# Two-layer decoder trunk: layer 0's first weight tiles on two queues, its keys gathered earlier, its gathered rows stored by GpSimd

## The chip, the cores and the metric

The kernel runs on one core of one Trainium2 chip. The metric is the device time of one execution in microseconds (us). A core has these engines: PE (TensorE, matmuls; PEld is its weight load), DVE (VectorE), ACT (ScalarE), POOL (GpSimd) and SP (SyncE). All data between DRAM and the on-chip memory, and from DRAM to DRAM, is moved by the core's 16 DMA engines. Three engines issue such transfers here, each into a queue of its own: SP (q1 in the profile), ACT (q10) and POOL (q0). Each queue is served in the order in which it was filled.

## What is computed

Two layers over 256 prompt positions and 8 sample rows which share the weights. Cut to what matters here (the function and variable names are the reference's):

```python
h = rms_norm(x, norm_g)
proj = jnp.einsum('btd,de->bte', h, w_in)            # 1024 -> 3200 columns
...                                                  # conv group, pooling group
kk = jnp.concatenate([k_buf, k], axis=1)             # cache of 2048 keys + the new one
vv = jnp.concatenate([v_buf, v], axis=1)
o = dilated_attention(q, kk, vv, k_buf.shape[1])     # dilations (1, 4, 16), 128 keys each
new_k = kk[:, -n_keep:]                              # the whole cache, shifted by one row
new_v = vv[:, -n_keep:]
y = jnp.einsum('bte,ed->btd', jnp.concatenate([ya, yb, yc], axis=-1), w_out)
```

The sample group's outputs `new_k` and `new_v` are the caches of both layers moved by one row: 8 samples, 2 layers, keys and values, 2048 rows of 1536 bytes each. That shifted copy is most of what the kernel moves.

## The kernel before, in words

**Weights.** There are 66 weight tiles of 128 rows of 4096 bytes (512 KB), 33 a layer: 25 projections (`PROJ`, in the order a_val and a_glu alternating, a_gate, q, k, v, c_gate, b_val, b_gate) and 8 output tiles. They go through a ring of `WRING = 14` buffers `wt`. SP issues tiles 0 to 13 at the start (L435), with most of the constants (`cst`, L437) behind the sixth; ACT issues tile n + 14 after it has drained projection n (`next_tile`, L786). PE multiplies tile by tile (L596 projections, L739 outputs) into three PSUM banks `pj`.

**Gathered rows.** Each layer's attention of the samples needs 20 slots of rows in `kg` (keys) and 20 in `vg` (values). `gather` issues 24 DMAs for each: 8 for the nearest rows (16 partitions x 4 slots, two rows of 1536 bytes in one piece of 3072: 64 pieces) and 16 for dilations 4 and 16 (16 x 6 slots of 1536 bytes: 96 pieces). DVE multiplies `kg` with the query `qb` (L1098, step `sscore`); in its order stands the rotary part of the next k tile (L1028 and after) behind the first of these products, and PE waits for that. PE reads `vg` in L668.

**The shifted copy.** POOL issues 96 copies from DRAM to DRAM (L511; three a sample: 256, 240 and 96 pieces of 4608 bytes; layer 1's first, then layer 0's) and 4 remainders (L515). They leave out the near rows and every fourth row of the part behind them; those come from `kg` and `vg`, by `put_back` (16 DMAs each: 8 with 64 pieces, 8 with 96), which SP issues (L406).

**SP's order, one instruction after the other.** x and constants, tiles, keys of layer 0, then in each layer: pool weights `pw`, `gather("v", l)` (its buffer `vg` holds x at the start; in layer 1 it waits until layer 0's values are stored), the states, `put_back` of the keys, parameters and states of the next layer, `gather("k", 1)` once layer 0's keys are used and stored, `put_back` of the values. At the end SP stores y and waits for all that is outstanding.

Of the kernel before, what the change touches and what calls it, by code (L numbers as in the profile page):

```python
# [37 lines left out]
PER_S = P // NS  # L38
# [7 lines left out]
GATHER = []  # L46
# [4 lines left out]
    _hi = _lo  # L51
SLOTS = sum(g[2] for g in GATHER)
NEW = SLOTS
SCORE_CUTS = [(a, a + 4) for a in range(0, SLOTS, 4)]


# [38 lines left out]
assert NRING % RING == 0  # L95

WRING = 14


CONV_TAPS = CONV_W * CT  # L100
# [79 lines left out]
          for a, b in ((0, 768), (768, EVEN_ROWS), (FAR_LO, GATHER[0][0]))]  # L180
NEAR_BYTES = 2 * C_ATT * 4
IN_FLIGHT = 16
assert DEPTH * len(COPIES) % IN_FLIGHT == 0
XROUNDS = 5

# [60 lines left out]
def trunk_program(nc, ins, const, const_at, outs):  # L246
    (y_prompt, y_sample, o_conv_p, o_pool_p, o_k_p, o_v_p, o_conv_s, o_pool_s, o_k_s, o_v_s) = outs
    with ExitStack() as ctx:
# [92 lines left out]
        for name, n in dict(  # L341

                par_in=10 * 16, st_in=2 * 16, pw_in=4 * 16, k_in=3 * NS * 16, v_in=3 * NS * 16,

                k_near_out=NS * 16, k_far_out=NS * 16, v_near_out=NS * 16, v_far_out=NS * 16, v_out=16, k_out=16, new_out=4 * 16, tail_out=4 * 16, state_out=2 * 16,

                pj_full=NRING, pj_free0=NRING // RING, pj_free1=NRING // RING, pj_free2=NRING // RING,
                tr_full=NTR, tr_free=NTR, st_full=NST, st_free=NST, rt_full=NRT, rt_free=NRT,
                sc_full=NH + 1, sc_free=NH + 1, o_full=NH, o_free=AT,

                xsq=KD, r_h_ok=1, h_ok=KD, qk_raw=2 * AT, qk_r=2 * AT, qk_ok=2 * AT,
                v_raw=AT, rep_ok=3, sig_ok=NGATES, u_ok=CT, sig_c_ok=AT, sig_a_ok=CT, sig_b_ok=PT_,
                nmax_ok=NH, p_raw=NH, p_ok=NH, kprod_ok=len(SCORE_CUTS), ks_used=len(SCORE_CUTS), ssub=1, sexp=1, spm_ok=1, so_ok=1,
                conv_ok=CONV_TAPS, yc_ok=1,
                ysq=1, rstd_ok=1, z_ok=1, ztanh=1, b_val_ok=PT_, pd_ok=1,
                mix_a=1, mix_b=PT_, mix_c=AT, mix_s=1, xT_ok=KD).items():
            S[name] = sem(name)
            per[name] = n
# [20 lines left out]
        def tile_of(g):  # L379

            return wt[:, g % WRING, :, :].rearrange("p k c -> p (k c)"), ins["w_tiles"][g // NRING, g % NRING], w_in[g % WRING]

        @block.sync
        def _(sp):
            def one(name, l):
                return ins[name][bass.ds(l, 1)]

            def gather(kind, l, to, name):

                at = 0  # L390
                for lo, d, n in GATHER:
                    for s in SAMPLE_ORDER:
                        rows = one(f"cache_{kind}_win", l)[:, s, lo:lo + d * n * PER_S]
                        rows = rows.rearrange("o (a b e) h d -> (o a) b e (h d)", a=PER_S, e=d)[:, :, 0, :]
                        sp.dma_start(to[sample_rows(s), at:at + n, :], rows, max_dma_last_dim=NEAR_BYTES).then_inc(S[name], 16)  # L395
                    at += n

            def put_back(l, to, frm, names):

                out = to[bass.ds(l, 1)]  # L400
                at = 0
                for (lo, d, n), name in zip(GATHER, names):
                    for s in SAMPLE_ORDER:
                        rows = out[:, s, lo - 1:lo - 1 + d * n * PER_S]
                        rows = rows.rearrange("o (a b e) h d -> (o a) b e (h d)", a=PER_S, e=d)[:, :, 0, :]
                        sp.dma_start(rows, frm[sample_rows(s), at:at + n, :], max_dma_last_dim=NEAR_BYTES).then_inc(S[name], 16)  # L406
                    at += n

            def params(l):
                sp.wait_ge(S["tr_full"], nth(l - 1, "tr_full", TR["par"] + 1))  # L410
# [19 lines left out]
            sp.dma_start(x_tok[0:NS, 2 * D_MODEL:3 * D_MODEL],  # L430
                         ins["x_sample"].rearrange("s t d -> (s t) d")).then_inc(x_in, 16)
            sp.dma_start(cst[:, 0:early], const[:, 0:early]).then_inc(early_in, 16)
            for g in range(WRING):
                buf, src, landed = tile_of(g)
                sp.dma_start(buf, src).then_inc(landed, 16)  # L435
                if g == 5:
                    sp.dma_start(cst[:, early:], const[:, early:]).then_inc(const_in, 16)  # L437

            for l in range(DEPTH):

                if l == 0:
                    gather("k", l, kg, "k_in")
                sp.wait_ge(zeroed, 1)
                if l > 0:
                    sp.wait_ge(S["rt_full"], nth(l, "rt_full", 0))
                for g in range(len(POOL_WINDOWS)):
                    r = 64 * (g % 2)
                    sp.dma_start(pw[r:r + 64, g // 2, r:r + 64], one("pool_w", l)[:, g].rearrange("o c d -> (o c) d"))\
                        .then_inc(S["pw_in"], 16)

                if l == 0:
                    sp.wait_ge(x_copied, XROUNDS)
                    sp.wait_ge(squared, 1)
                else:
                    sp.wait_ge(S["sc_full"], nth(l - 1, "sc_full", NH + 1))
                    for name in ("v_near_out", "v_far_out"):
                        sp.wait_ge(S[name], nth(l - 1, name, per[name]))
                sp.wait_ge(S["pj_full"], nth(l, "pj_full", PIDX[("a_gate", 0)]))
                gather("v", l, vg, "v_in")
                for name, out, keep in (("state_conv", o_conv_s, TAIL - 1), ("state_pool", o_pool_s, POOL_BUF - 1)):  # L460
                    sp.dma_start(out[bass.ds(l, 1), :, 0:keep].rearrange("o s w c -> (o s) (w c)").rearrange("s (e x) -> e s x", e=16),
                                 one(name, l)[:, :, 1:keep + 1].rearrange("o s w c -> (o s) (w c)").rearrange("s (e x) -> e s x", e=16))\
                        .then_inc(S["state_out"], 16)

                sp.wait_ge(S["k_in"], nth(l, "k_in", per["k_in"]))
                sp.wait_ge(S["pj_full"], nth(l, "pj_full", PIDX[("v", 0)]))
                put_back(l, o_k_s, kg, ("k_near_out", "k_far_out"))
                if l < DEPTH - 1:
                    params(l + 1)
                    states(l + 1)  # L470
                    sp.wait_ge(S["ks_used"], nth(l, "ks_used", len(SCORE_CUTS)))
                    for name in ("k_near_out", "k_far_out"):
                        sp.wait_ge(S[name], nth(l, name, per[name]))
                    gather("k", l + 1, kg, "k_in")
                sp.wait_ge(S["v_in"], nth(l, "v_in", per["v_in"]))
                put_back(l, o_v_s, vg, ("v_near_out", "v_far_out"))
            y_rows = y_prompt.rearrange("b (r p) d -> r p (b d)", p=P)
            sp.wait_ge(y_copied, 1)
            sp.dma_start(y_rows[0][:, 0:512], y_tok[:, 0:512]).then_inc(y_out, 16)
# [8 lines left out]
            sp.wait_ge(bulk_out, 16 * 4)  # L488
            for i in range(IN_FLIGHT):
                sp.wait_ge(copy_out[i], 16 * DEPTH * len(COPIES) // IN_FLIGHT)  # L490
            for name in ("k_near_out", "k_far_out", "v_near_out", "v_far_out", "v_out", "k_out", "new_out", "tail_out", "state_out"):
                sp.wait_ge(S[name], DEPTH * per[name])
            sp.wait_ge(y_out, 80)

# [1 line left out]
        def _(pool):  # L496
# [4 lines left out]
            for l in reversed(range(DEPTH)):  # L501
                for i, (kind, s, a, b) in enumerate(COPIES):
                    n = (DEPTH - 1 - l) * len(COPIES) + i
                    cache, out = (ins["cache_k_win"], o_k_s) if kind == "k" else (ins["cache_v_win"], o_v_s)
                    if a < FAR_LO:
                        dst = out[l, s, a:b].rearrange("(c e r) h d -> c e (r h d)", c=16, r=PIECE_ROWS)
# [251 lines left out]
        def _(act):  # L758
# [9 lines left out]
            for r0, name in ((ROW_QN, "q_norm_g"), (ROW_KN, "k_norm_g")):  # L768
                for h in range(2):
                    act.dma_start(prow[r0:r0 + 1, h * HD:(h + 1) * HD], ins[name][bass.ds(0, 1)]).then_inc(S["par_in"], 16)  # L770

            act.wait_ge(x_in, 32)
            act.wait_ge(early_in, 16)
            unused = hT[:, :, :].rearrange("p k c -> p (k c)")
# [3 lines left out]
            A(mix[0:NS, :, :].rearrange("p k c -> p (k c)")[:, 0:D_MODEL], x_tok[0:NS, 2 * D_MODEL:3 * D_MODEL], ACT.Square,  # L778
              accum_out=x_sum[0:NS, 2:3]).then_inc(squared, 1)
            act.wait_ge(squared, 1)  # L780

            def next_tile(g):

                if g < DEPTH * NRING:
                    buf, src, landed = tile_of(g)
                    act.dma_start(buf, src).then_inc(landed, 16)  # L786

            act.dma_start(st_conv[:, :, :], ins["state_conv"][bass.ds(0, 1)].rearrange("o (r s) w c -> (o s w) r c", r=2)
                          ).then_inc(S["st_in"], 16)
            act.dma_start(st_pool[:, :], ins["state_pool"][bass.ds(0, 1)].rearrange("o s w c -> (o s w) c")).then_inc(S["st_in"], 16)  # L790
            for l in range(DEPTH):
                def rsqrt_of(dst, src, scale, free_n, ok_sem, n):

# [5 lines left out]
                for step in ACT_SCHEDULE:  # L799
# [17 lines left out]
                    elif kind == "proj":  # L817
# [30 lines left out]
                        elif group == "b_val":  # L848
                            nc.scalar.copy(p_ext[:, t, POOL_BUF:], src[:, 0:SEQ])
                            nc.scalar.copy(p_smp[:, t, :, POOL_BUF], src[:, SEQ:T]).then_inc(S["b_val_ok"], 1)  # L850
                            act.wait_ge(S["b_val_ok"], nth(l, "b_val_ok", t + 1))
                            act.sem_inc(free, 1)
                        next_tile(l * NRING + n + WRING)
                    elif kind == "norm":
                        i = step[1]
# [409 lines left out]
```

## Time and profile before

| what | us |
|---|---|
| median of three runs | 409.22 (408.93 to 413.0) |
| the profiled execution, device time | 406.74 |
| its span, first to last instruction | 404.9 |
| PE busy | 336.8 |
| DVE busy | 232.5 |
| ACT busy | 99.3 |
| POOL busy | 54.2 |

All times in the rows are us from the start of the span. The profiled execution lies 2.5 us below the median of the three runs, and 1.8 us lie around its span. The page gives the busy time of each engine, the span in 40 slices with the share in which the 16 DMA engines were busy and the rate in GB/s, the DMA queues, and the chain of work that ended last. A DMA queue's "packets" are the pieces that it moved, with the small ones that report a transfer's end. SPq, ACTq and POOL's DMA rows are the times in which those engines issue transfers.

### The profile page before, as it was taken

How to read it: one execution, taken by the hardware profiler on the slowest of the kernel's cores; microseconds unless marked ns; L12 is line 12 of the kernel's file. 1: busy time of each engine (PE TensorE's matmuls, PEld its weight loads, DVE VectorE, ACT ScalarE, POOL GpSimd, SP SyncE). 2: the span in 40 equal slices, each digit the busy share in tenths (PEclk: the TensorE clock that was granted, in tenths of full speed). 3: DMA queues.
4: the chain of work that ended last, by engine and by line, in shares of the span. 5: the costliest groups of instructions: out<-in, count | busy, mean ns of one | idle time of the engine just before them, and what ended most of it. 6: DMA issues, size and time to landing. Idle time of an engine off the chain costs nothing.

```text
span 404.9 us, 4681 instructions
## 1 busy us (share of the span) xinstructions
PE 336.8 (83%) x1546; PEld 267.5 (66%) x1546; DVE 232.5 (57%) x524; ACT 99.3 (25%) x234; POOL 54.2 (13%) x104
## 2 busy tenths in 40 slices
PE   1799999920557897898997999999778996989991
PEld 1588888810435675667886888888556765758881
DVE  1625798401998578753103358988988587662101
ACT  2300215410023333251102001353214332340011
POOL 2710101111111111111011110111111011200000
PEclk9999999975595999999999999999867999999997
DMA  7999999999999999999999999999999999999995
GB/s 289 417 419 419 419 418 416 416 415 379 363 396 394 395 404 414 411 367 393 415 418 417 412 417 418 415 414 386 416 416 383 387 375 399 359 399 359 345 330 196
DMA packets 51269, 158.10 MB, mean 390 GB/s; under 512 B 6356, under 2 KB 18078, under 8 KB 51246
## 3 DMA queue, kind: packets, MB, share of 16 engines
q0 software_dynamic: 21056, 89.61, 56.7%
q1 hardware_dynamic: 20804, 38.60, 25.8%
q10 hardware_dynamic: 9386, 29.60, 18.3%
q8 instruction: 12, 0.20, 0.2%
q14 instruction: 11, 0.09, 0.1%
HBM read 143.91 MB, written 104.42 MB: 613 GB/s over the span
## 4 chain that ended last, share of the span: by engine, by line
PE 49%; DVE 19%; SPq 18%; DMA 6%; ACT 3%; issue 3%; ACTq 0%; DVEq 0%
PE pj L596 21%; PE pj L739 14%; SPq L395 14%; DMA kg<-in_cache_k_win 6%; DVE yc L1157 4%; SPq L435 4%; PE psc L668 4%; DVE tok L1098 3%; DVE ssc L1101 3%; PE ptr L521 3%; DVE spsum_pad L1127 1%; PE ps L716 1%; PE ps L555 1%; ACT sc L903 1%; DVE sc L1065 1%
## 5 line engine op out<-in xcount | busy, mean ns | idle before, releaser
L596 PE MATMUL pj<-hT,wt 128*128 128x264 f32 x800 | 194.1, 401 | 3.0 <-DVE hT L1017 3.0
L596 PEld LDWEIGHTS pj<-hT,wt 128*128 128x128 f32 x800 | 156.6, 199 | 34.7 <-issue 7.3
L1157 DVE SCALAR_TENSOR_TENSOR yc<-u_ext,par,yc 128x256 f32<-128x256 f32 x180 | 76.2, 480 | 2.8 <-DVE u_smp L1045 0.6
L739 PE MATMUL pj<-mix,wt 128*128 128x264 f32 x256 | 59.4, 387 | 0.0
L739 PEld LDWEIGHTS pj<-mix,wt 128*128 128x128 f32 x256 | 48.0, 190 | 7.9
L511 POOL DMA_DIRECT2D out<-in_cache_v_win x48 | 25.8, 544 | 166.0 <-issue 166.0
L511 POOL DMA_DIRECT2D out<-in_cache_k_win x48 | 26.0, 549 | 119.4 <-issue 111.8
L1227 DVE TENSOR_TENSOR xT<-xT,pj 128x264 f32<-128x264 f32 x16 | 6.9, 430 | 53.5 <-PE pj L739 53.5
L1098 DVE TENSOR_TENSOR tok<-kg,qb 128x1536 f32<-128x1536 f32 x10 | 17.6, 1758 | 23.4 <-DMA kg<-in_cache_k_win 22.9
L608 PE MATMUL prt<-sqg,cst 128*128 128x264 f32 x24 | 7.9, 415 | 22.2 <-DVE scr L1028 22.2
L844 ACT ACTIVATE ex<-pj 128x264 f32<-128x264 f32 x22 | 8.6, 391 | 69.6 <-PE pj L596 56.0
L608 PEld LDWEIGHTS prt<-sqg,cst 128*128 128x128 f32 x24 | 4.7, 200 | 23.3 <-DVE scr L1028 22.6
L1101 DVE TENSOR_REDUCE ssc<-tok 128x24 f32<-128x1536 f32 x10 | 17.5, 1753 | 0.3
L521 PE MATMUL ptr<-cst,sc 128*128 128x128 f32 x36 | 7.0, 310 | 12.3 <-DVE sc L1076 12.3
L802 ACT ACT_TABLE_LOAD x12 | 15.4, 1283 | 1.6 <-ACT sqg L831 0.9
L1043 DVE SCALAR_TENSOR_TENSOR u_ext<-ex,pj 128x256 f32<-128x256 f32 x6 | 2.5, 422 | 22.2 <-ACT ex L844 22.2
L668 PE MATMUL psc<-vg,spm_pad 128*64 128x384 f32 x80 | 15.2, 502 | 0.0
L521 PEld LDWEIGHTS ptr<-cst,sc 128*128 128x128 f32 x36 | 4.4, 153 | 16.0 <-DVE sc L1076 15.6
L1052 DVE SCALAR_TENSOR_TENSOR mix<-ex,pj 128x264 f32<-128x264 f32 x16 | 6.9, 428 | 9.5 <-ACT ex L844 9.3
L951 ACT ACTIVATE hT<-xT 128x264 f32<-128x264 f32 x8 | 3.4, 422 | 31.7 <-DVE xT L1227 31.7
L901 ACT ACTIVATE sc<-sc,nmax 128x128 f32<-128x128 f32 x12 | 4.8, 401 | 25.2 <-DVE nmax L1069 19.3
L835 ACT COPY vT<-pj 128x264 f32<-128x264 f32 x6 | 2.3, 379 | 35.4 <-PE pj L596 35.3
(175 smaller groups left out, 329.3 us busy)
## 6 DMA issues: line engine op xcount, KB each, us to landing
wt<-in_w_tiles ACTq DMA_DIRECT2D x52, 512.0 KB, 8.1
out<-in_cache_k_win POOLq DMA_DIRECT2D x16, 1152.0 KB, 66.2
out<-in_cache_v_win POOLq DMA_DIRECT2D x16, 1152.0 KB, 61.4
out<-in_cache_k_win POOLq DMA_DIRECT2D x17, 1080.0 KB, 70.7
out<-in_cache_v_win POOLq DMA_DIRECT2D x17, 1080.0 KB, 64.7
wt<-in_w_tiles SPq DMA_DIRECT2D x14, 512.0 KB, 21.6
out<-in_cache_k_win POOLq DMA_DIRECT2D x16, 432.0 KB, 72.5
out<-in_cache_v_win POOLq DMA_DIRECT2D x16, 432.0 KB, 66.7
```

Of the source, the lines that this page charges most:

```text
L395: sp.dma_start(to[sample_rows(s), at:at + n, :], rows, max_dma_last_dim=NEAR_BYTES).then_inc(S[name], 16)
L435: sp.dma_start(buf, src).then_inc(landed, 16)
L511: pool.dma_start(dst, src, max_dma_last_dim=PIECE_ROWS * C_ATT * 4).then_inc(copy_out[n % IN_FLIGHT], 16)
L521: return nc.tensor.transpose(out, in_, C["ident"][0:rows, 0:rows])
L596: last = nc.tensor.matmul(pj[n % RING][:, 0:T], wt[:, g % WRING, k, :], hT[:, k, :], start=(k == 0), stop=(k == KD - 1))
L608: nc.tensor.matmul(prt[:, 0:T], C["rot"], qg[:, i % 2, :], start=True, stop=True).then_inc(S["rt_full"], 1)
L668: nc.tensor.matmul(psc[o:o + SV_HALF, 0:C_ATT], spm_pad[:, j * NH * NS:j * NH * NS + SV_HALF], v, start=(j < 2), stop=(j >= SLOTS - 1))
L739: last = nc.tensor.matmul(pj[n % RING][:, 0:T], wt[:, g % WRING, k, :], mix[:, k, :], start=(k == 0), stop=(k == KD - 1))
L802: nc.scalar.preload_act_table_set(TABLE_BEFORE[step])
L1098: V.tensor_tensor(tok[:, :, :], kg[:, a:b, :], qb[:, None, :].to_broadcast([P, b - a, C_ATT]), ALU.mult).then_inc(S["kprod_ok"], 1)
L1101: last = V.tensor_reduce(ssc[:, a:b, :], tok[:, :, :].rearrange("p j (h d) -> p j h d", h=NH), AX.X, ALU.add)
L1157: last = V.scalar_tensor_tensor(out=yc[:, t, 0:SEQ], in0=x_w, scalar=par[:, ROW_CW + w * CT + t:ROW_CW + w * CT + t + 1], in1=yc[:, t, 0:S ...
```

## The change

Four edits. SP issues only tiles 0 to 3, then the 8 near gathers of layer 0's keys, then the constants, then the 16 others. ACT issues tiles 4 and 5 before it waits for x, tiles 6 to 9 behind the first states, and 10 to 13 after it has drained projection 0. `put_back` takes the engine that issues it; for layer 0 that is POOL, which stores the keys ahead of its 25th copy and the values ahead of its 49th, each behind a wait for the gather (`k_in`, `v_in`). Layer 1's rows are stored by SP as before, on semaphores of their own.

```diff
+SP_TILES, ACT_TILES = 4, (6, 10)
+STORED = {"k": 3 * NS, "v": 6 * NS}
...
-            for g in range(WRING):
+            for g in range(SP_TILES):
                 buf, src, landed = tile_of(g)
                 sp.dma_start(buf, src).then_inc(landed, 16)
-                if g == 5:
-                    sp.dma_start(cst[:, early:], const[:, early:]).then_inc(const_in, 16)
+            gather("k", 0, kg, "k_in", GATHER[:1])
+            sp.dma_start(cst[:, early:], const[:, early:]).then_inc(const_in, 16)
+            gather("k", 0, kg, "k_in", GATHER[1:])
...
-                if l == 0:
-                    gather("k", l, kg, "k_in")
...
-                sp.wait_ge(S["k_in"], nth(l, "k_in", per["k_in"]))
-                sp.wait_ge(S["pj_full"], nth(l, "pj_full", PIDX[("v", 0)]))
-                put_back(l, o_k_s, kg, ("k_near_out", "k_far_out"))
+                if l > 0:
+                    sp.wait_ge(S["k_in"], nth(l, "k_in", per["k_in"]))
+                    put_back(sp, l, o_k_s, kg, ("k_near_last", "k_far_last"))
...
-                sp.wait_ge(S["v_in"], nth(l, "v_in", per["v_in"]))
-                put_back(l, o_v_s, vg, ("v_near_out", "v_far_out"))
+                if l > 0:
+                    sp.wait_ge(S["v_in"], nth(l, "v_in", per["v_in"]))
+                    put_back(sp, l, o_v_s, vg, ("v_near_last", "v_far_last"))
...
+                    if n == STORED["k"]:
+                        pool.wait_ge(S["k_in"], nth(0, "k_in", per["k_in"]))
+                        put_back(pool, 0, o_k_s, kg, ("k_near_out", "k_far_out"))
+                    elif n == STORED["v"]:
+                        pool.wait_ge(S["v_in"], nth(0, "v_in", per["v_in"]))
+                        put_back(pool, 0, o_v_s, vg, ("v_near_out", "v_far_out"))
...
+            for g in range(SP_TILES, ACT_TILES[0]):
+                next_tile(g)
             act.wait_ge(x_in, 32)
...
+            for g in range(*ACT_TILES):
+                next_tile(g)
...
+                        if l == 0 and n == 0:
+                            for g in range(ACT_TILES[1], WRING):
+                                next_tile(g)
                         next_tile(l * NRING + n + WRING)
```

SP's first instructions before (`vg` holds x at the start, `kg` the gathered keys, `wt` the weight tiles; the numbers behind are partitions, slots and elements):

```order
L428 DMA vg<-in_x_prompt 128x2x1024
L430 DMA vg<-in_x_sample 8x1024
L432 DMA cst<-in_const 128x129
L435 DMA wt<-in_w_tiles 128x1024 x6
L437 DMA cst<-in_const 128x1279
L435 DMA wt<-in_w_tiles 128x1024 x8
L395 DMA kg<-in_cache_k_win 16x4x768 x8
L395 DMA kg<-in_cache_k_win 16x6x384 x16
```

And SP's first instructions of the change:

```order
L431 DMA vg<-in_x_prompt 128x2x1024
L433 DMA vg<-in_x_sample 8x1024
L435 DMA cst<-in_const 128x129
L438 DMA wt<-in_w_tiles 128x1024 x4
L410 DMA kg<-in_cache_k_win 16x4x768 x8
L440 DMA cst<-in_const 128x1279
L410 DMA kg<-in_cache_k_win 16x6x384 x16
```

Ten tiles have gone from SP's queue, and the near keys stand ahead of the constants. ACT's part of the change, from its first tile on (`prow` and `st_*` are parameters and states, `ex` the gate of projection 1):

```order
L780 DMA prow<-in_k_norm_g 1x64 x2
L786 DMA wt<-in_w_tiles 128x1024 x2
L794 ACTIVATE hT,x_sum<-vg 128x1024 x2
L796 ACTIVATE mix,x_sum<-vg 8x1024
L799 DMA st_conv<-in_state_conv 120x2x384
L801 DMA st_pool<-in_state_pool 120x256
L786 DMA wt<-in_w_tiles 128x1024 x4
L807 ACTIVATE r_h<-ps,cst 128x264
L809 ACTIVATE r_h<-r_h 128x264
L815 ACT_TABLE_LOAD
L786 DMA wt<-in_w_tiles 128x1024 x5
L857 ACTIVATE ex<-pj1 128x264
```

The ten tiles stand in three places, the last four with tile 14 in one run of five ahead of `ex`. POOL's row in the change where its copies of layer 1's keys end and those of the values begin:

```order
L521 DMA out<-in_cache_k_win 96x1152
L395 DMA out<-kg 16x4x768 x8
L395 DMA out<-kg 96x1x384 x8
L521 DMA out<-in_cache_v_win 256x1152
```

The 16 stores of the keys have moved from SP to here; the 16 of the values stand in the same way ahead of the copies of layer 0.

## Rows read from the trace of the kernel before

**Rows 1.** The page's DMA and PE lines over the span's 40 slices.
```profile
PE   1799999920557897898997999999778996989991
...
DMA  7999999999999999999999999999999999999995
GB/s 289 417 419 419 419 418 416 416 415 379 363 396 394 395 404 414 411 367 393 415 418 417 412 417 418 415 414 386 416 416 383 387 375 399 359 399 359 345 330 196
DMA packets 51269, 158.10 MB, mean 390 GB/s; under 512 B 6356, under 2 KB 18078, under 8 KB 51246
```
**Rows 2.** The page's DMA queues over the span: POOL's q0, SP's q1, ACT's q10.
```profile
q0 software_dynamic: 21056, 89.61, 56.7%
q1 hardware_dynamic: 20804, 38.60, 25.8%
q10 hardware_dynamic: 9386, 29.60, 18.3%
...
HBM read 143.91 MB, written 104.42 MB: 613 GB/s over the span
```
**Rows 3.** Timeline of POOL's issues: start, length, line, transfer, idle time before.
```profile
61.20 1.61 POOL L511 DMA_DIRECT2D out<-in_cache_v_win  x3 [15.18 <-issue]
...
154.63 1.61 POOL L511 DMA_DIRECT2D out<-in_cache_k_win  x3 [11.75 <-issue]
...
348.50 1.07 POOL L515 DMA_DIRECT2D out<-in_cache_v_win  x2
```
**Rows 4.** The page's DMA issues: KB each, median us from issue to landing.
```profile
out<-in_cache_v_win POOLq DMA_DIRECT2D x16, 1152.0 KB, 61.4
...
out<-kg SPq DMA_DIRECT2D x16, 192.0 KB, 24.5
```
**Rows 5.** DMA queues in 378 to 394 us: packets, MB, share.
```profile
DMA packets 1507, 5.27 MB, mean 329 GB/s; under 512 B 134, under 2 KB 289, under 8 KB 1507
...
q0 software_dynamic: 1075, 4.57, 88.5%
q1 hardware_dynamic: 432, 0.70, 14.9%
```
**Rows 6.** Waits of SP's queue over the span: total, times, longest.
```profile
SPq L457 <- DMA out<-vg: 19.7, 1, 19.7
SPq L483 <- ACT hT L962: 11.5, 1, 11.5
SPq L473 <- DMA out<-kg: 8.3, 1, 8.3
SPq L493 <- DMA out<-qk: 4.8, 1, 4.8
```
**Rows 7.** Timeline of DVE: start, length, line, form, idle time before it.
```profile
76.66 0.56 DVE L1058 COPY qb<-ptr 128x384 f32<-128x384 f32 x1
100.11 1.76 DVE L1098 TENSOR_TENSOR tok<-kg,qb 128x1536 f32<-128x1536 f32 x1 [22.89 <-DMA kg<-in_cache_k_win]
```
**Rows 8.** Stretches: PE, PEld, DVE, ACT, POOL busy, PEclk, DMA share, GB/s.
```profile
20.00:80.00 60.00, 60.00 (x277) 50.90 (x276) 39.87 (x100) 14.72 (x36) 6.47 (x12) 1.00 1.03 418
...
100.00:112.00 12.00, 6.29 (x18) 4.87 (x18) 11.65 (x16) 0.00 (x0) 1.63 (x3) 0.58 1.01 366
112.00:180.00 68.00, 56.12 (x271) 40.93 (x271) 51.16 (x111) 23.58 (x62) 9.68 (x18) 0.92 1.03 398
180.00:280.00 100.00, 96.71 (x449) 80.68 (x448) 52.53 (x130) 21.59 (x49) 12.94 (x25) 1.00 1.03 412
280.00:380.00 100.00, 88.21 (x405) 66.28 (x404) 66.89 (x141) 28.00 (x71) 10.28 (x20) 0.91 1.03 386
...
394.00:400.00 6.00, 2.74 (x15) 1.85 (x13) 1.12 (x2) 1.05 (x2) 0.00 (x0) 1.00 0.88 329
```
**Rows 9.** DMA queues in 40 to 70 us.
```profile
q0 software_dynamic: 1221, 5.23, 42.4%
q10 hardware_dynamic: 1194, 4.23, 34.5%
q1 hardware_dynamic: 1221, 3.03, 25.4%
```
**Rows 10.** DMA queues in 0 to 10 us.
```profile
q1 hardware_dynamic: 885, 2.82, 76.7%
```
**Rows 11.** DMA queues in 10 to 40 us.
```profile
q1 hardware_dynamic: 1406, 5.24, 42.9%
q0 software_dynamic: 1174, 5.07, 41.0%
q10 hardware_dynamic: 857, 2.21, 18.5%
```
**Rows 12.** Timeline of SP's issues.
```profile
5.56 13.21 SPq L435 DMA_DIRECT2D wt<-in_w_tiles  x8
18.81 58.56 SPq L395 DMA_DIRECT2D kg<-in_cache_k_win  x24
```
**Rows 13.** Timeline of ACT around its first tile issue.
```profile
23.41 0.37 ACTq L786 DMA_DIRECT2D wt<-in_w_tiles  x1
26.97 0.39 ACT L844 ACTIVATE ex<-pj 128x264 f32<-128x264 f32 x1 [8.65 <-PE pj L596]
```
**Rows 14.** The chain that ended last: start, length, engine, line.
```profile
166.09 2.58 PE psc L668 x15
...
278.39 1.77 DVE tok L1098
...
345.34 2.82 PE psc L668 x15
...
396.98 0.59 ACT hT L962
```
**Rows 15.** DMA queues in 77 to 100 us, all together.
```profile
DMA packets 3285, 9.25 MB, mean 402 GB/s; under 512 B 585, under 2 KB 1568, under 8 KB 3285
```

More of the change, by code:

```diff
@@ L53 @@
 NEW = SLOTS
+SLOT_OF = {g[1]: sum(h[2] for h in GATHER[:i]) for i, g in enumerate(GATHER)}
 SCORE_CUTS = [(a, a + 4) for a in range(0, SLOTS, 4)]
@@ L343, in trunk_program @@
                 par_in=10 * 16, st_in=2 * 16, pw_in=4 * 16, k_in=3 * NS * 16, v_in=3 * NS * 16,
-                k_near_out=NS * 16, k_far_out=NS * 16, v_near_out=NS * 16, v_far_out=NS * 16, v_out=16, k_out=16, new_out=4 * 16, tail_out=4 * 16, state_out=2 * 16,
+                k_near_out=NS * 16, k_far_out=NS * 16, v_near_out=NS * 16, v_far_out=NS * 16,
+                k_near_last=NS * 16, k_far_last=NS * 16, v_near_last=NS * 16, v_far_last=NS * 16, v_out=16, k_out=16, new_out=4 * 16, tail_out=4 * 16, state_out=2 * 16,
                 pj_full=NRING, pj_free0=NRING // RING, pj_free1=NRING // RING, pj_free2=NRING // RING,
@@ L381, in tile_of, with put_back @@
             return wt[:, g % WRING, :, :].rearrange("p k c -> p (k c)"), ins["w_tiles"][g // NRING, g % NRING], w_in[g % WRING]
+        def put_back(eng, l, to, frm, names):
+            out = to[bass.ds(l, 1)]
+            at = 0
+            for (lo, d, n), name in zip(GATHER, names):
+                for s in SAMPLE_ORDER:
+                    rows = out[:, s, lo - 1:lo - 1 + d * n * PER_S]
+                    rows = rows.rearrange("o (a b e) h d -> (o a) b e (h d)", a=PER_S, e=d)[:, :, 0, :]
+                    eng.dma_start(rows, frm[sample_rows(s), at:at + n, :], max_dma_last_dim=NEAR_BYTES).then_inc(S[name], 16)
+                at += n
         @block.sync
@@ L386, in one, with gather @@
                 return ins[name][bass.ds(l, 1)]
-            def gather(kind, l, to, name):
-                at = 0
-                for lo, d, n in GATHER:
+            def gather(kind, l, to, name, spans=GATHER):
+                for lo, d, n in spans:
+                    at = SLOT_OF[d]
                     for s in SAMPLE_ORDER:
@@ L395, in gather @@
                         sp.dma_start(to[sample_rows(s), at:at + n, :], rows, max_dma_last_dim=NEAR_BYTES).then_inc(S[name], 16)
[L396 to L407, printed above, removed]
             def params(l):
@@ L490, in _ @@
                 sp.wait_ge(copy_out[i], 16 * DEPTH * len(COPIES) // IN_FLIGHT)
-            for name in ("k_near_out", "k_far_out", "v_near_out", "v_far_out", "v_out", "k_out", "new_out", "tail_out", "state_out"):
+            for name in ("k_near_out", "k_far_out", "v_near_out", "v_far_out", "k_near_last", "k_far_last", "v_near_last", "v_far_last"):
+                sp.wait_ge(S[name], per[name])
+            for name in ("v_out", "k_out", "new_out", "tail_out", "state_out"):
                 sp.wait_ge(S[name], DEPTH * per[name])
@@ L770, in _, with next_tile @@
                     act.dma_start(prow[r0:r0 + 1, h * HD:(h + 1) * HD], ins[name][bass.ds(0, 1)]).then_inc(S["par_in"], 16)
+            def next_tile(g):
+                if g < DEPTH * NRING:
+                    buf, src, landed = tile_of(g)
+                    act.dma_start(buf, src).then_inc(landed, 16)
+            for g in range(SP_TILES, ACT_TILES[0]):
+                next_tile(g)
             act.wait_ge(x_in, 32)
@@ L780, in _ @@
             act.wait_ge(squared, 1)
[L782 to L786, printed above, removed]
             act.dma_start(st_conv[:, :, :], ins["state_conv"][bass.ds(0, 1)].rearrange("o (r s) w c -> (o s w) r c", r=2)
```

## Prediction, made before the changed kernel ran

> **What bounds the kernel now.** The page's 40 slices come first. PE has a hole in slices 9 to 11 and again near slice 29, so PE alone isn't the bound; the DMA line stands at 9 (90% or more) from the second slice to the last but one [rows 1]. The reader is to see that the 16 DMA engines have something to do from about 10 us until 400 us, whatever the compute engines do. The queues say what: 89.61 of 158.10 MB are POOL's copies from DRAM to DRAM, each byte of which is read and written, hence 143.91 MB read and 104.42 written [rows 2]. POOL issues its last copy at about 349 us, and a copy takes some 61 us from issue to landing [rows 3, 4]: 349 + 61 = 410, so the copies run to the very end. In 378 to 394 us q0 has 88.5% of the engines' time, long after the last weight tile [rows 5]. So two things end together: the chain of compute, whose last y store SP waits for (4.8 us) [rows 6], and the copies.
>
> The waits come next. The largest on the chain of compute is DVE's for layer 0's gathered keys: the query copy at 76.66 us is done at 77.2, the product starts at 100.11, 22.89 us later [rows 7]. Everything behind it is late by that.
>
> The stretches show that the DMA engines are full at different rates: 418 GB/s in 20 to 80 us, when the tile queue is active beside the copies; 366 in 100 to 112, when all 14 buffers have filled up during DVE's wait; 412 in 180 to 280; 386 in 280 to 380; and 329 when the copies are nearly alone [rows 5, 8]. The share is about 1.0 in each, so what differs is what the pieces cost: copies want loads beside them.
>
> **Edits at the start: when do the keys land?** In 40 to 70 us all three queues have work, and their packets are 1221, 1221 and 1194 [rows 9]: the engines take a piece from each queue in turn, whatever its size. So what counts for the keys is the number of pieces ahead in SP's queue. Before: 264 for x, 256 for constants, 14 x 128 for tiles, 8 x 64 + 16 x 96 = 2048 for keys, 4360 in all, and 16 small ones for each of 42 DMAs: 5032. The change takes out ten tiles with 10 x (128 + 16) = 1440, leaving 3592. By 10 us 885 had passed [rows 10]; tiles 4 and 5 now run on ACT's queue at that time, so I take off half of their 256 pieces, leaving 757. The remaining 2835 at 1406 / 30 = 46.9 per us [rows 11] take 60 us, at 1221 / 30 = 40.7 per us [rows 9] 70 us. The keys land between 70 and 80 us; the upper end is the likelier, since ACT's queue is now full from the start, and a transfer's last engine may be some us behind the mean. They are needed at 77.2. Of the 22.9 us of wait I take 20 as gone, with 15 and 22.9 as ends.
>
> The weight tiles: ACT's queue gets its turns too. A tile is 144 packets, so 3.1 to 3.5 us at these rates; tile 6 is issued near 12 us and PE needs it some 22 us after its first. They come in time. ACT's run of five tiles at about 23.4 us can block ACT, as SP's eight tiles took 13.21 us to issue when its queue was full [rows 12]; `ex` at 26.97 stands behind them [rows 13]. By that row a blocked tile costs 13.21 / 8 = 1.65 us on average, 8 us for five, against 0.37 for one that finds room; between 0 and 8, I take 3, most of it covered by the three `pj` banks, and it is hidden anyway if the copies set the end.
>
> **POOL's stores.** POOL reaches copy 24 at 61.20 and copy 48 at 154.63 us [rows 3]. The wait for the keys holds it from 61 until 80; its queue holds 61 us of copies, so the DMA engines don't run dry: cost nothing, cover 61 against 19. Without that cover it would be the 19. The values are gathered right behind the keys (2048 + 24 x 16 pieces at 40.7 per us: 60 us, so by 140); PE reads them at 166 before, which becomes 146 [rows 14]. Each store set adds 16 x 0.54 us of issue on POOL (1.61 / 3 for one), hidden in waits of 11 to 15 us. What it moves is time of landing: instead of 24.5 us from issue a store now takes about 61 [rows 4]. Keys: issued from 80, landed by 145; layer 1's keys are needed at 278 - 20 = 258 [rows 14]. Values: issued near 165, landed by about 230; SP waited 19.7 us for this store before, until 277 [rows 6], so this comes earlier. Behind it are the values of layer 1, needed at 345 - 20 = 325 [rows 14]. No term.
>
> **The sum.** Compute ends 20 us earlier, near 377 instead of 397 [rows 14], and its y stores by 385. But the bytes are the same 158.10 MB. In those 20 us the engines moved 402 GB/s [rows 15], 8.0 MB. These have to be moved at the end instead, by copies alone: 8.0 / 0.329 [rows 5] = 24.4 us. That is +4.4 us. Against it stands the stretch of full buffers: 12 us at 366 become a stretch like 180 to 280 at 412 [rows 8], 12 x (412 - 366) / 412 = 1.3 us back. Sum +3.1 us. The other bound: the 8.0 MB spread over the late stretch at 386: 20.7 us, +0.7, less 1.3, -0.6. Between -0.6 and +3.1 I take +1.5: some of the loads and stores that now lie beside copies (SP's 25.8%) stay beside them. Span 404.9 + 1.5 = 406.4, device time 408.2 by the profiled execution. That execution is 2.5 us below the median of 409.22, so for a median: 410.7.
>
> HBM's own limit can be weighed here. In 378 to 394 us, 88% of a 329 GB/s stretch is copies, which is about 2 x 0.29 + 0.04 = 0.62 TB/s read and written [rows 5]. The Trainium skill (HBM Reference, Specifications (TRN2)) gives about 716 GB/s for the memory that two cores share. By that figure copies alone would do 358 GB/s, the 8.0 MB 22.4 us, and the sum would be +1.1 us; the trace shows less than the page's figure in that stretch, and the sum above goes by the trace.
>
> **Rivals.**
>
> 1. *The copies decide, at no price or a small one* (0.50), as above: 410.7, own range 406 to 413.
>
> 2. *Slower: the copies alone are dearer than I take.* Compute is out of the way for the full 22.9 us, 9.25 MB are moved at the end at 329 GB/s: 28.1 us, +5.2 with nothing given back: 414.4. In 394 to 400 us the DMA share already falls to 0.88 [rows 8], engines finish unevenly, and a longer stretch of copies alone may spread them further. For it: the last stretches fall from 359 to 330 GB/s [rows 1]. Against: the gather of the values beside copies without tiles ran at 366, and that goes away. It decides from +4.1 us on, that is 8.0 MB moved below 332 GB/s with nothing regained. 0.25.
>
> 3. *Faster: the mix gets better.* Stores in POOL's queue take turns in place of copies, not beside them, and tiles flow steadily. If 112 to 180 us went from 398 to 412 GB/s that is 68 x 14 / 412 = 2.3 us, and 280 to 380 from 386 to 400, 3.5 us: -5.8, 403.4. For it: every stretch with tiles shows 412 to 418. Against: layer 1's stores stay where they are, and what pauses the tiles there is DVE, not the keys. 0.20.
>
> 4. *The change doesn't bring the keys forward.* They would land near 100 and the time stays 409.2. Against: equal turns [rows 9], with 1440 packets less ahead. 0.05. The Trainium skill (DMA: Bandwidth & Descriptors, Issuing engines are not separate DMA queues) says that issuing from several engines only saves sequencer time, the transfers sharing the same 16 engines. Taken alone that gives this case; the trace's equal packet counts of three queues speak against it for one queue's landing, and for it where the sum of all bytes is meant.
>
> If DMA did not bind, the time would be 409.2 - 20 = 389; the DMA line leaves that no chance beyond what the range's low end cuts off.
>
> **How the numbers follow.** About 1% (4.1 us) is what a measurement of this kernel can tell from no change. Case 3 lies mostly on the faster side, with a little of case 1: 0.22. Case 2 mostly slower, with a little of case 1: 0.27. The rest, 0.51, is the same. The range takes in 403 (case 3) and 416 (case 2 with the spread of the runs before): 402.5 to 416.5.
>
> **What would show it.** In the profile after: DVE's wait for the keys (before its first product with `kg`) below 8 us, with keys landed by 85; PE's last matmul near 375 to 380; q0 nearly alone, at 320 to 345 GB/s, for the last 20 to 30 us rather than 15; SP's last wait for a copy, not for the y store; DMA share 9 to the last slice. Wrong if the 16 DMA engines show idle time in the middle (POOL's queue dry behind a wait), if a tile is late in 20 to 80 us, or if the copies at the end run above 360 GB/s: then the time falls below 405.

## The result, and the profile after

Over 20 runs each, the kernel before took 409.11 us (median) and the changed kernel 412.86 us. The ratio is 1.0104, with a 95% interval of 1.0084 to 1.0124: the change costs about 1%, or 4.3 us. The forecast was 410.7 us with no measurable change as the likeliest; the sign and the range (402.5 to 416.5) hold, and the time lies between the likeliest case and the slower rival. The profiled execution has a span of 411.5 us against 404.9; it lies 0.5 us above its median and the one before 2.4 us below, so the two traces show more difference than the medians.

The first look goes to the page's slices of the changed kernel (PE's busy tenths, the DMA engines' busy tenths, GB/s).

```profile
PE   2799999976999698999799999878896998994000
...
DMA  8999999999999999999999999999999999999992
GB/s 292 415 418 414 418 415 415 417 418 415 416 400 411 413 416 388 395 414 416 393 381 421 412 390 419 413 416 389 380 400 372 398 369 347 328 342 340 347 321 81
```

PE's hole in slices 9 to 11 of [rows 1] is gone, and PE has nothing left to do in the last three slices, some 31 us. The DMA line stays at 9 to the last slice but one. What was gained in compute lies idle at the end.

DVE's timeline shows that the wait for the keys went entirely (start, length, line, form; no idle time stands behind the product):

```profile
77.38 0.56 DVE L1074 COPY qb<-ptr 128x384 f32<-128x384 f32 x1
78.07 1.76 DVE L1114 TENSOR_TENSOR tok<-kg,qb 128x1536 f32<-128x1536 f32 x1
```

Against [rows 7] the product starts 22.04 us earlier. The waits of SP's queue show what now ends last:

```profile
SPq L458 <- DMA out<-vg: 58.1, 1, 58.1
...
SPq L492 <- DMA out<-in_cache_v_win: 27.6, 1, 27.6
...
SPq L474 <- DMA out<-kg: 5.0, 1, 5.0
```

In [rows 6] the last wait was 4.8 us for a y store (the samples' y lies in the buffer that the row calls `qk`). Now it is 27.6 us for copies from DRAM to DRAM (L492). In the middle SP stands 58.1 us until the values' store by POOL has landed, against 19.7 before.

The stretches answer to [rows 8] (PE, PEld, DVE, ACT, POOL busy, clock, DMA share, GB/s):

```profile
20.00:80.00 60.00, 60.00 (x272) 50.77 (x272) 41.35 (x101) 14.49 (x35) 7.01 (x14) 1.00 1.03 416
...
100.00:112.00 12.00, 10.23 (x36) 7.43 (x36) 9.48 (x18) 4.79 (x12) 1.19 (x3) 0.72 1.03 416
112.00:180.00 68.00, 62.03 (x316) 46.73 (x315) 38.03 (x97) 19.83 (x47) 15.76 (x30) 1.00 1.03 404
180.00:280.00 100.00, 92.34 (x407) 76.72 (x407) 67.93 (x144) 23.18 (x56) 16.62 (x31) 0.96 1.03 407
...
340.00:380.00 40.00, 33.56 (x165) 27.86 (x163) 6.88 (x19) 2.58 (x5) 5.18 (x10) 0.98 1.02 339
```

The stretch at 366 GB/s is now at 416, as forecast. In this trace what is lost comes late: 339 GB/s from 340 us on, against 373 in the kernel before. The queues in 345 to 400 us (packets, MB, share of the engines):

```profile
DMA packets 4769, 18.54 MB, mean 337 GB/s; under 512 B 406, under 2 KB 485, under 8 KB 4768
...
q0 software_dynamic: 4079, 17.32, 94.6%
q1 hardware_dynamic: 689, 1.20, 6.4%
```

Copies are nearly alone there for 55 us. Before that was so in some 20 us, from 380 on. It is tempting to take this for the whole price; the experiments below don't bear that out.

### The profile page after: what moved, and what is told of

Its sections match the earlier page's. It is cut to its first block, busy times and chain, and to the rows that moved or that the text cites. A ratio compares the mean times of both kernels' runs of the same rounds, so it can differ in the third digit from the quotient of the medians.

```text
span 411.5 us, 4681 instructions
## 1 busy us (share of the span) xinstructions
PE 337.2 (82%) x1546; PEld 267.8 (65%) x1546; DVE 232.4 (56%) x524; ACT 99.3 (24%) x234; POOL 70.6 (17%) x136
## 2 busy tenths in 40 slices
DMA packets 49732, 158.09 MB, mean 384 GB/s; under 512 B 6356, under 2 KB 16542, under 8 KB 49710
## 3 DMA queue, kind: packets, MB, share of 16 engines
q0 software_dynamic: 22592, 95.12, 60.2%
## 4 chain that ended last, share of the span: by engine, by line
PE 63%; DVE 20%; ACT 4%; issue 2%; DMA 2%; ACTq 0%; SPq 0%; DVEq 0%
PE pj L606 34%; PE pj L749 14%; DVE yc L1173 4%; PE psc L678 3%; DVE tok L1114 3%; DVE ssc L1117 3%; PE ptr L531 3%; DMA cst<-in_const 2%; DVE spsum_pad L1143 1%; PE psc L531 1%; PE ps L726 1%; PE ps L565 1%; ACT sc L919 1%; DVE sc L1081 1%; PE po L663 1%
## 5 line engine op out<-in xcount | busy, mean ns | idle before, releaser
L395 POOL DMA_DIRECT2D out<-kg x16 | 8.2, 521 | 31.2 <-DMA kg<-in_cache_k_win 31.0
L395 POOL DMA_DIRECT2D out<-vg x16 | 8.2, 520 | 20.1 <-issue 20.1
L644 PE MATMUL psc<-qk 64*128 64x128 f32 x24 | 6.7, 366 | 5.9 <-DVE qk L1048 5.9
```

Of the source, the lines that this page charges most:

```text
L395: eng.dma_start(rows, frm[sample_rows(s), at:at + n, :], max_dma_last_dim=NEAR_BYTES).then_inc(S[name], 16)
```

## The experiments

Each ratio is against runs of the kernel before on the same chip. Its median there was 411.91 us beside the start alone, POOL's stores alone, the last 24 copies on SP and the first kernel with larger pieces; 408.18 beside the later stores, all stores by POOL and the last two kernels; 409.31 beside the rest. So the ratios are to be compared, not the times.

**Do the copies decide?** Two kernels leave the 48 copies of layer 0 out, in the kernel before and in the changed one. They lack that part of the computation's output: q0 moves 45.96 MB in place of 89.61 in the first, so 43.7 MB are left out (the 42.6 of the expectation counts a MB as 1000 KB of 1024 bytes).

```diff
-                    pool.dma_start(dst, src, max_dma_last_dim=PIECE_ROWS * C_ATT * 4).then_inc(copy_out[n % IN_FLIGHT], 16)
+                    if l > 0:
+                        pool.dma_start(dst, src, max_dma_last_dim=PIECE_ROWS * C_ATT * 4).then_inc(copy_out[n % IN_FLIGHT], 16)
```

(with the final wait for half as many.) Expected of the kernel before without them:

> The kernel before without the 48 copies of layer 0 (they are left out, 42.6 of 158 MB). The DMA engines are then no longer busy to the end. If compute is the second bound, the time stays that of its chain with DVE's wait for the keys in it: 400 to 408. If the copies didn't decide, it would be as before, 409.

And of the changed kernel without them:

> The changed kernel without the same 48 copies. If the early keys shorten compute and the copies were what hid it, this lies 18 to 23 us under the run without them of the kernel before: 380 to 388. If the new start brings nothing even where DMA is free, both are alike within 3 us.

Measured in one run each: 408.69 and 382.05 us. The page of the second one:

```profile
PE   1799999996789969999979999999676996999995
...
DMA  8999999999999999999999999999982001000011
```

PE works to the end and the DMA engines stop in slice 31. Where the engines have room, the changed kernel is 26.6 us faster, by one run each and more than the 18 to 23 us expected; in the full kernel it can bring none of that. The kernel before stood at two bounds at once: with 43.7 MB less it is as slow (408.69 against 409.31).

**Which edit costs?** First the new start alone; layer 0's rows are stored by SP again:

```diff
-                        pool.wait_ge(S["k_in"], nth(0, "k_in", per["k_in"]))
-                        put_back(pool, 0, o_k_s, kg, ("k_near_out", "k_far_out"))
...
-                if l > 0:
-                    sp.wait_ge(S["k_in"], nth(l, "k_in", per["k_in"]))
-                    put_back(sp, l, o_k_s, kg, ("k_near_last", "k_far_last"))
+                sp.wait_ge(S["k_in"], nth(l, "k_in", per["k_in"]))
+                sp.wait_ge(S["pj_full"], nth(l, "pj_full", PIDX[("v", 0)]))
+                put_back(sp, l, o_k_s, kg, ("k_near_last", "k_far_last") if l else ("k_near_out", "k_far_out"))
```

(the values likewise. The wait for `pj_full`, which the change had taken out, comes back for both layers; SP never stands at it in this trace.)

> The changed kernel with its new start (tiles on two queues, keys early), but layer 0's gathered rows stored by SP as before. Theory 'copies last': the price comes from compute, and with it the loads, leaving the copies alone at the end; it belongs to the early keys. Then this is dear too: 410 to 413, copies alone for the last 50 us or so, no wait of DVE for the keys. Rival 'POOL's stores': the price comes from POOL standing 31 us at the keys and from stores taking turns of the copies. Then this has none of it: 405 to 409.

Measured: 411.27 us, ratio 0.9987 (0.9948 to 1.0026). The time falls into the first theory's span only because this chip was slow for the kernel before too; by the ratio the start alone costs nothing, between 2.1 us gained and 1.1 lost. DVE doesn't wait for the keys, yet the stretch of copies nearly alone is not the expected 50 us. SP's queue still moves gathered rows beside them until about 378 us (346 in the changed kernel); these are the queues in 340 to 380 us, with the start alone and then in the changed kernel:

```profile
DMA packets 4729, 14.53 MB, mean 363 GB/s; under 512 B 552, under 2 KB 1622, under 8 KB 4728
...
q1 hardware_dynamic: 2153, 3.70, 26.9%
```
```profile
DMA packets 3620, 13.55 MB, mean 339 GB/s; under 512 B 312, under 2 KB 632, under 8 KB 3619
...
q1 hardware_dynamic: 693, 1.07, 8.3%
```

The other half, POOL's stores behind the old start, was:

```diff
-            for g in range(SP_TILES):
+            for g in range(WRING):
...
-            gather("k", 0, kg, "k_in", GATHER[:1])
-            sp.dma_start(cst[:, early:], const[:, early:]).then_inc(const_in, 16)
-            gather("k", 0, kg, "k_in", GATHER[1:])
+                if g == 5:
+                    sp.dma_start(cst[:, early:], const[:, early:]).then_inc(const_in, 16)
+            gather("k", 0, kg, "k_in")
```

(and no tile of the first 14 on ACT.)

> The changed kernel with the start of the kernel before (14 tiles on SP, keys behind them), and the stores of layer 0's gathered rows by POOL. Copies last: DVE's wait for the keys of about 23 us is back, compute ends near 397, copies alone only for the last 15 to 20 us: within 2 us of the kernel before, 407 to 411. POOL's stores: POOL now waits at its 25th copy until the keys land near 100, longer than in the changed kernel, so it should be dearer than the changed kernel: 413 to 418.

Measured: 416.58 us, ratio 1.0100 (1.0067 to 1.0134). The stores carry the whole price, with either start. That speaks against the theory that the price belongs to the early keys. It isn't the rival's picture in full either: POOL's wait for the keys was longer here, as expected, and the price no higher; 416.58 us lies in the rival's 413 to 418 only because of the slower chip.

```profile
101.13 8.40 POOL L395 DMA_DIRECT2D out<-kg  x16 [55.32 <-DMA kg<-in_cache_k_win]
```

POOL stood 55.32 us in this kernel, and 31.04 in the changed one.

**Is it POOL's standing?** The stores are moved back in POOL's order:

```diff
-STORED = {"k": 3 * NS, "v": 6 * NS}
+STORED = {"k": 5 * NS - 4, "v": 8 * NS - 4}
```

> The changed kernel with POOL's stores of layer 0 placed later among its copies: keys ahead of the 37th copy, values ahead of the 61st, so that POOL doesn't stand at the keys any more (it stood 31 us). Theory 'displaced turns': a store in POOL's queue uses turns that copies had, the copies get that much later, and are left alone at the end. Then nothing changes in the price: 1.0 to 1.3% above the kernel before. Rival 'POOL's standing': its 31 us wait lets its queue thin out, and that is the price. Then it falls by most of 1%, to within 0.3% of the kernel before.

Measured: 412.65 us, ratio 1.0101 (1.0057 to 1.0144). POOL no longer waits for the keys, and the price is the same. That rival falls.

But so does half of the theory that it was set against. The queues in 345 to 400 us of this kernel:

```profile
DMA packets 6439, 19.88 MB, mean 362 GB/s; under 512 B 741, under 2 KB 2124, under 8 KB 6438
...
q0 software_dynamic: 3560, 15.09, 76.5%
q1 hardware_dynamic: 2832, 4.76, 25.9%
```

Here SP's queue works beside the copies until about 384 us, much as in the kernel before (355 GB/s, q1 at 24.7% in the same stretch), and yet the kernel is 1% slower. Its weakest stretch against the kernel before lies earlier: 112 to 180 us at 385 GB/s against 398, with q1 at 9.9% against 24.0%, while SP stood 44.4 us for POOL's store of the keys and later 69.1 us for that of the values. So copies left alone at the end are not what the price hangs on.

**One store at a time.** Only the keys by POOL, or only the values, with the other pair by SP (the edits are the halves of the one that made the start alone).

> The changed kernel with only layer 0's keys stored by POOL, its values by SP. If each stored byte in POOL's queue costs alike (displaced turns), half the price: 0.4 to 0.6% above the kernel before. If the price is the 58 us in which SP stands empty until POOL's store of the values has landed, none: within 0.3% of the kernel before.

> The changed kernel with only layer 0's values stored by POOL, its keys by SP. Displaced turns: half the price, 0.4 to 0.6% above the kernel before. SP standing empty for the values' store: the whole price, 0.8 to 1.2% above it.

Measured: keys 412.62 us, 1.0058 (1.0024 to 1.0092); values 413.03 us, 1.0073 (1.0039 to 1.0107). Each costs about half. SP's 58 us without work are in neither trace: its wait ahead of layer 1's values is 19.7 us with the keys by POOL and 22.6 us with the values by POOL (an execution of 416.42 us, above that kernel's median). The values cost 0.73% without the wait, so the wait isn't the price; it goes with the stores themselves.

**Twice as many.** All four sets by POOL, layer 1's keys ahead of the 73rd copy and its values ahead of the 89th:

```diff
+                    elif n == 9 * NS:
+                        pool.wait_ge(S["k_in"], nth(1, "k_in", per["k_in"]))
+                        put_back(pool, 1, o_k_s, kg, ("k_near_last", "k_far_last"))
+                    elif n == 11 * NS:
+                        pool.wait_ge(S["v_in"], nth(1, "v_in", per["v_in"]))
+                        put_back(pool, 1, o_v_s, vg, ("v_near_last", "v_far_last"))
```

(and SP's stores of layer 1 are taken out.)

> The changed kernel with layer 1's gathered rows stored by POOL too (keys ahead of the 73rd copy, values ahead of the 89th), none by SP: twice the stored bytes in POOL's queue. Displaced turns: the price grows with the bytes, another 0.7 to 1.2%, to about 2% above the kernel before; the stretch in which only copies are left begins near 310 us instead of 345. If the price belongs to layer 0's place (the wait for the keys, or the 58 us in which SP has nothing to issue), no more than 0.3% is added.

Measured: 413.64 us, ratio 1.0129 (1.0085 to 1.0172). That is 0.25% over the changed kernel where 0.7 to 1.2 were expected; the intervals are wide enough to hold 0.7, but the centre is far below. The amount in the late place is not settled. The stretch without SP's queue did come, and earlier than expected; the queues in 300 to 340 us:

```profile
q0 software_dynamic: 3355, 13.79, 98.6%
q10 hardware_dynamic: 336, 0.43, 2.9%
```

By the queues in steps of 3 us, SP's last gathered rows end at these times:

| kernel | SP's last gathered rows, us | ratio |
|---|---|---|
| all stores by POOL | 295 | 1.0129 |
| changed kernel | 346 | 1.0104 |
| POOL's stores, old start | 361 | 1.0100 |
| later stores | 384 | 1.0101 |
| start alone | 378 | 0.9987 |

Behind that time the copies are nearly alone. The stretch varies by 90 us among the four kernels with POOL's stores, and their prices lie within 0.3%; the start alone has it as the later stores do and pays nothing. So its length isn't what the stores cost.

What POOL's timeline shows of the displaced copies: the 49th copy, layer 0's first, was issued at 154.63 us before [rows 3]. In the changed kernel it is this row:

```profile
193.51 0.56 POOL L521 DMA_DIRECT2D out<-in_cache_k_win  x1 [3.51 <-issue]
...
359.11 1.07 POOL L525 DMA_DIRECT2D out<-in_cache_v_win  x2
```

With the start alone:

```profile
163.58 1.61 POOL L518 DMA_DIRECT2D out<-in_cache_k_win  x3 [8.97 <-issue]
...
357.83 1.07 POOL L522 DMA_DIRECT2D out<-in_cache_v_win  x2
```

And with all stores by POOL, the last copies:

```profile
370.29 1.07 POOL L525 DMA_DIRECT2D out<-in_cache_v_win  x2 [1.05 <-issue]
```

The 49th copy is 39 us later than before, 30 us later than with the start alone. By the last issue most of that has been caught up (359 against 358). The two profiled executions, 411.5 and 411.1 us of span, don't show the difference that the medians show; the execution profiled of the start alone lies above its own median. So the price of the stores is measured by the ratios, and the way from stores in POOL's queue to a late end is not shown. One rival was not run: the same stores in a third queue, ACT's. So whether they cost because they share a queue with the copies, or because POOL issues them, is open.

**Is it the queue or DRAM that holds copies alone at 340 GB/s?** The last 24 copies are issued by SP behind its last store:

```diff
+                    if l == 0 and kind == "v":
+                        continue
...
+                sp.dma_start(dst, src, max_dma_last_dim=PIECE_ROWS * C_ATT * 4).then_inc(tail_copied, 16)
```

> The changed kernel with the last 24 of the 96 copies (layer 0's values) issued by SP after its last store of gathered rows, so that two queues hold copies at the end. If the rate of copies alone (about 340 GB/s) is a limit of reading and writing DRAM, it stays at 330 to 350 GB/s with two queues, and the time is 411 to 415. If it is a limit of a single queue, the rate rises to 380 to 418 and the time falls by 5 to 10 us, to 403 to 408.

Measured: 416.48 us, ratio 1.0090 (1.0050 to 1.0130), within the changed kernel's interval. The stretches:

```profile
280.00:340.00 60.00, 52.10 (x249) 37.85 (x248) 42.12 (x98) 20.98 (x55) 0.00 (x0) 0.91 1.03 378
340.00:380.00 40.00, 37.55 (x186) 30.22 (x184) 9.85 (x24) 5.11 (x8) 0.00 (x0) 1.00 1.01 326
```

And the queues in 345 to 390 us:

```profile
DMA packets 3464, 14.73 MB, mean 327 GB/s; under 512 B 262, under 2 KB 273, under 8 KB 3463
...
q1 hardware_dynamic: 3463, 14.72, 100.8%
```

POOL's queue had run dry by about 340 us, so this is not two queues at once but copies alone on SP's queue instead of POOL's. Their rate is 327 GB/s there and 337 on POOL's. So it isn't a limit of POOL's queue. The time of this kernel says less, since SP issues the y stores only behind its copies, from 392.73 us on. Whether two queues of copies at once would do more wasn't reached.

**Can the mix be bettered?** Larger pieces in the copies outside the strided part:

```diff
+                    rows = PIECE_ROWS if a >= FAR_LO else 6 if a == 0 else 5
```

(used for the pieces in place of `PIECE_ROWS`.)

> The changed kernel with larger pieces in the copies (9216 and 7680 bytes in place of 4608 outside the strided part; same bytes). Queues take turns piece by piece, so the copies get more bytes per turn while loads run, and less is left for the end. Copies last: the stretch of copies alone shrinks from 60 us to under 30, compute ends 10 to 25 us later, and the time falls to 403 to 410 as long as compute stays under it. Rival: the copies cost the same wherever they lie, so the time stays at 411 to 414. Too much: keys and tiles get so late that compute sets the end, above 414.

Measured: 414.29 us, ratio 1.0049 (1.0010 to 1.0089). That is 0.5% better than the changed kernel, though the two intervals just touch, and 0.5% slower than the one before. In 340 to 380 us it moved 358 GB/s instead of 339, and PE's work ended near 395 us instead of 375. This is an execution of 410.22 us, 4 us below that kernel's median:

```profile
340.00:380.00 40.00, 37.95 (x196) 28.50 (x197) 17.37 (x45) 7.89 (x11) 0.78 (x2) 1.00 1.03 358
```

The direction is the expected one, the size smaller. POOL stood 72.9 us at the keys and 36.3 us at the values in this trace, so SP's small pieces had got late. Then the start alone with pieces of 4 and 5 rows, and the same without POOL's first wait:

```diff
-                        put_back(pool, 0, o_k_s, kg, ("k_near_out", "k_far_out"))
...
+                    rows = PIECE_ROWS if a >= FAR_LO else 4 if a == 0 else 5
```

> The new start alone (stores by SP, as in the run on the start alone), and larger pieces in the copies: 6144 and 7680 bytes in place of 4608 outside the strided part. More of the copies is done in their turns while loads run, and compute, which ended some 25 us before the copies, is delayed by less than that. Displaced turns, read the other way: 0.5 to 1.2% below the kernel before. If the copies' bytes cost the same everywhere: within 0.3% of it.

```diff
-            pool.wait_ge(x_in, 32)
```

> The run before this with POOL's first copies not held back until x has landed (that wait ended at 7.3 us). The engines get copies some 5 us earlier, x lands 1 to 4 us later, and compute has that to spare: 0.2 to 0.6% below the run with the wait. If the start of compute still decides the end: 0.3 to 0.8% above it.

Both are far slower than expected: 435.03 us, ratio 1.0644 (1.0591 to 1.0697), and 438.22 us, 1.0724 (1.0682 to 1.0765). The second lies 0.75% above the first, as its alternative had it (0.3 to 0.8%), but the intervals touch and compute bounds both, so it says little. The page of the first one names the cause in its chain, and its GB/s line shows idle engines at the end; below it stands the wait in 330 to 380 us:

```profile
GB/s 295 416 419 417 419 415 419 419 418 420 419 418 390 415 395 397 406 398 419 421 382 418 417 417 419 419 401 372 366 354 416 366 347 376 360 311 199 2 48 52
...
SPq 63%; DMA 22%; PE 12%; issue 2%; DVE 0%; ACT 0%; ACTq 0%; DVEq 0%
```
```profile
PE psc L676 <- DMA vg<-in_cache_v_win: 27.9, 1, 27.9
```

With larger pieces in POOL's queue, each turn of SP's small ones takes longer. SP carries all stores here, so its chain of gathers and stores got later (it issues layer 1's values at 314.66 us, with the start alone at 267.22), until PE waited 27.9 us for them and compute came back as the bound. None of the versions is measurably faster than the kernel before.

## Why the prediction was right, and where its steps failed

**The bound.** Right. That the copies run to the end was read from slices, queues and the last issue; the two kernels with half the copies show it, and that compute was a second bound at the same place.

**When the keys land.** The count of turns gave 70 to 80 us. POOL, which waits for just that, goes on at 76.19 us. The queues in 40 to 70 us of the changed kernel show equal turns again:

```profile
q0 software_dynamic: 1356, 5.75, 46.6%
q10 hardware_dynamic: 1354, 4.90, 40.1%
q1 hardware_dynamic: 1356, 1.79, 16.2%
```

Of the wait 22.9 us went, where 20 were taken. The rival that the keys are not brought forward falls. The Trainium skill (DMA: Bandwidth & Descriptors, Issuing engines are not separate DMA queues) says that issuing on several engines only saves the issuing engine's time. For one queue's landing the runs differ from that; for the sum of the bytes the trace agrees, 158.10 and 158.09 MB in engines that were full in both.

**ACT's issues.** The run of five tiles took 2.27 us where 3 were taken, and the gate `ex` came at 27.69 instead of 26.97 us [rows 13]. Hidden, as said.

**The sum.** This is where it was right by luck in part. The +1.5 us were worked out for the early keys: 8.0 MB moved at the end at 329 GB/s, less the stretch that came back. Both rates came out near (337 GB/s for the copies alone, and 416 where 412 was taken). But the start alone measures -0.5 us (-2.1 to +1.1), so the term was too high, its lower bound (-0.6) the better one. Loads and stores that had been beside copies mostly stayed there: in 340 to 380 us SP's queue moved 3.70 MB with the start alone and 4.05 before.

**POOL's stores: "No term".** This step failed. Standing was rightly costed at nothing (the run with later stores), and the later landing did no harm to compute (PE ends near 375 us, as forecast). But the ratios of the start alone and of the changed kernel differ by 1.2%, some 4.8 us. The working counted issue time, waits and landings; it never counted that 5.5 MB had changed queue, and that the copies behind them, which set the end, stand in that queue. That the stores cost this is shown; by what way is not, and twice the bytes added only 0.25%. The third rival even named it as a gain (stores in place of copies, not beside them), and it was a loss. The second rival, slower, had about the right total, 414.4, by a mechanism that belonged to the wrong edit.

**What would show it.** Keys by 85, PE done by 380, copies nearly alone at 320 to 345 GB/s, the last wait one for a copy: all seen. The DMA share falls in the last slice, and the copies were nearly alone for some 60 us rather than 20 to 30.

## What to carry to other kernels

Before costing a removed wait, ask whether the DMA engines were full to the last slice: if they were, the wait's 22.9 us are worth nothing, and the same change was worth 26.6 us once they weren't (one run each). Then find the queue whose last transfer ends the kernel, and don't put at nothing what an edit moves into it, even where its issue and its landing cost nothing: here 5.5 MB of stores cost about 1%. Don't take a stretch that looks bad in one trace for the cause before a second variant shows it: the later stores cost the same without it. Queues shared the engines turn by turn here (1356, 1354 and 1356 packets in 30 us), so the pieces ahead of a transfer in its own queue gave its landing, and larger pieces in POOL's queue made SP's late.

## What the runs showed of the hardware

Copies from DRAM to DRAM alone or nearly alone ran at 327 GB/s on SP's queue and 337 on POOL's (94.6% of the engines' time), against 416 to 418 in 20 to 80 us with weight tiles beside them. Each byte of a copy is both read and written in DRAM.

POOL's queue moves the same stores in fewer packets. This is the page's queue table of the start alone, in which SP stores them:

```profile
q0 software_dynamic: 21056, 89.61, 56.5%
q1 hardware_dynamic: 19364, 33.35, 22.3%
```

And of the changed kernel:

```profile
q0 software_dynamic: 22592, 95.12, 60.2%
q10 hardware_dynamic: 10826, 34.85, 21.1%
q1 hardware_dynamic: 16292, 27.85, 18.5%
```

5.5 MB left q1 with 3072 packets and came to q0 with 1536. So a store took about half as many turns in POOL's queue as in SP's. Nor did it take more of the engines' time: q0 gained about 15.5 us of it (60.2% of 411.5 less 56.5% of 411.1), and q1 lost as much. Both speak for a smaller price than was measured, so the way to it stays open.
